# A two-layer decoder trunk on one core: who keeps the last token pairs, splits the gates and does the first u chunks of the spreading stage

## The reference

```python
q = einsum('td,dn->tn', x, wq)                      # 512 tokens, 8 heads, two halves
s1, s2 = q_half @ keys                              # 128 keys per half
v1, i1 = top_k(s1, 16); v2, i2 = top_k(s2, 16)
top_s, pos = top_k(v1[..., :, None] + v2[..., None, :], 16)
eidx = i1 * 128 + i2 at pos                         # 8 heads x 16 experts per token, of 16384
gate = softmax(top_s)
hidden = gelu(einsum('td,thkd->thk', x, u_tab[eidx]))
y = einsum('thk,thkd->td', gate * hidden, v_tab[eidx])
```

## Time and profile before

| | |
|---|---|
| time, median of 3 | 3749.36 us |
| the profiled execution, its own time | 3750.3 us |
| its span, first to last instruction | 3748.6 us |
| mean granted TensorE clock | 0.995 |
| spreading, layer 1 | about 940 to 1117 us of the span |
| spreading, layer 2 | about 2804 to 2981 us |

### The profile page before, as it was taken

How to read it: one execution, slowest core, us unless ns; L and a number is a source line. 1 busy time by engine, 2 the same in 40 slices (tenths; PEclk the granted TensorE clock), 3 DMA queues, 4 the chain that set the end, 5 groups by cost and what they waited for, 6 DMA issues and landing times. The chain is left out here.

```text
span 3748.6 us, 53748 instructions
## 1 busy us (share of the span) xinstructions
PE 3673.4 (98%) x20234; PEld 3258.1 (87%) x20234; DVE 2775.9 (74%) x4663; ACT 1488.8 (40%) x2178; POOL 1017.2 (27%) x654
## 2 busy tenths in 40 slices
PE   9999999999999999999999999999999999999999
PEld 7878888999899999888888787889999989998887
DVE  5256635499988888898862665355999798888997
ACT  2254522344763333333322545232447643333332
POOL 1000000265004555555100000002640055555541
PEclk9999999999999999999999999999999999999999
DMA  4312524354689999999832225233547899999996
GB/s 157 118 63 71 172 84 141 110 187 159 217 256 368 369 362 334 361 407 391 305 129 95 73 68 172 76 141 114 203 150 231 276 357 360 361 342 362 405 394 240
DMA packets 323828, 860.19 MB, mean 229 GB/s; under 512 B 21056, under 2 KB 119360, under 8 KB 298432
## 3 DMA queue, kind: packets, MB, share of 16 engines
q1 hardware_dynamic: 249920, 589.39, 44.0%
q0 software_dynamic: 73728, 268.47, 18.8%
HBM read 763.41 MB, written 94.37 MB: 229 GB/s over the span
## 5 line engine op out<-in xcount | busy, mean ns | idle before, releaser
L97 PE MATMUL bank<-xT_low,u_high 128*128 128x384 f32 (+1 forms) x2144 | 730.2, 341 | 19.4 <-DVEq L2104 9.5
L99 PE MATMUL bank<-xT_high,u_low 128*128 128x384 f32 (+1 forms) x2144 | 724.1, 338 | 0.0
L98 PE MATMUL bank<-xT_high,u_high 128*128 128x384 f32 (+1 forms) x2144 | 723.8, 338 | 0.0
L97 PE MATMUL bank<-v_low,w_high 128*128 128x512 f32 x1536 | 598.3, 389 | 0.4 <-DVE v_low L2131 0.3
L99 PE MATMUL bank<-v_high,w_low 128*128 128x512 f32 x1536 | 598.1, 389 | 0.0
L98 PE MATMUL bank<-v_high,w_high 128*128 128x512 f32 x1536 | 598.0, 389 | 0.0
L1325 POOL DMA_INDIRECT far_rows<-peer_u_rows_dram,far_index x256 | 369.8, 1444 | 690.5 <-DVE far_dots L1331 638.6
L1257 POOL TENSOR_TENSOR u_low<-merged,u_high 128x1024 fp32r<-128x1024 f32 x96 | 243.6, 2552 | 1098.5 <-ACT u_high L1252 1098.4
L1325 POOL DMA_INDIRECT far_rows<-peer_v_dram,far_index x256 | 385.2, 1505 | 338.9 <-DVE x_far L1349 290.4
L2043 ACT ACTIVATE v_high<-v_raw 128x1024 fp32r<-128x1024 f32 x256 | 257.1, 1052 | 453.0 <-PE bank L99 391.1
L97 PEld LDWEIGHTS bank<-xT_low,u_high 128*128 128x128 f32 x2144 | 404.3, 189 | 26.4 <-DVEq L2104 10.1
(11 more groups left out here) (451 smaller groups left out, 6772.3 us busy)
## 6 DMA issues: line engine op xcount, KB each, us to landing
merged<-peer_u_dram SPq DMA_DIRECT2D x128, 1024.0 KB, 8.0
v_raw<-peer_v_dram SPq DMA_DIRECT2D x128, 1024.0 KB, 9.1
gates_scratch<-stage SPq DMA_DIRECT2D x24, 2048.0 KB, 8.4
G<-gates_scratch SPq DMA_DIRECT2D x64, 768.0 KB, 8.2
hidden_scratch<-ahead_hid SPq DMA_DIRECT2D x72, 384.0 KB, 2.6
hid<-hidden_scratch SPq DMA_DIRECT2D x36, 768.0 KB, 8.4
mg_raw<-w_merge_dram SPq DMA_DIRECT2D x28, 768.0 KB, 4.2
merged<-w_in_dram SPq DMA_DIRECT2D x20, 1024.0 KB, 6.3
```

The source lines that it names most:

```text
L97: nc.tensor.matmul(out, lh, rl, start=first, stop=False)
L98: nc.tensor.matmul(out, lh, rh, start=False, stop=False)
L99: return nc.tensor.matmul(out, ll, rh, start=False, stop=last)
```

## The change

It has four parts, all at the two ends of spreading; every instruction's arithmetic stays what it was.

1. The copies of the last tile's pairs move from the end of routing into spreading, on ACT behind the high half of chunk 2 and ahead of the first one-hot rows. `pairs_kept` tells DVE (which waits for it before the `find` of step 16, the last tile's first) and GpSimd.
2. GpSimd, which had nothing in spreading, splits the gates of the first tile, makes `u_low` of chunks 2 and 3, and splits the gates of the other two tiles.
3. PE, ACT and DVE have u's chunks half a chunk to a chunk earlier: PE does all of chunk 2 and half of chunk 3 in step 0, then the second half of chunk n + 2 and the first half of chunk n + 3; nothing stands behind step 23, and step 23 itself has one half chunk. DVE's `low` of chunk n + 3 stands in step n from step 1 on (behind `weigh` in step 1, ahead of it from step 2). ACT's `high` of chunk n + 4 opens step n, that of chunk 4 closes step 0.
4. Each gelu is one step earlier, and with it the store of its hidden values; `keep_pairs` counts one signal per tile where it counted six.

The core of the diff:

```diff
+def keep_turned_pairs(nc, bank, rowT, listed, gateT, gate_part, t):
+
+    A = nc.scalar.activation
+    tokens = slice((t - 1) * P, t * P)
+    steps = slice((t - 1) * P // STEP, t * P // STEP)
+    by_step = bank[3][:].rearrange("p (v n s) -> p v n s", v=4, s=STEP)
+    gates = bank[3][:, 2 * P:3 * P]
+    A(rowT[:, steps, :], by_step[:, 0, :, ROWS_BY_ACT], ACT.Copy)
+    for v, first, last, at in ((1, 0, STEP, 0), (0, 0, ROWS_BY_ACT.start, STEP), (0, ROWS_BY_ACT.stop, STEP, STEP + ROWS_BY_ACT.start)):
+        A(listed[:, steps, at:at + last - first, :],
+          by_step[:, v, :, first:last].unsqueeze(3).to_broadcast([P, P // STEP, last - first, 2]), ACT.Copy)
+    A(gateT[:, tokens], gates, ACT.Copy)
+    return A(gate_part[:, tokens, :], gates.unsqueeze(2).to_broadcast([P, P, 2]), ACT.Copy)
+
+
 def route_stage(nc, a, layer, sb, sem, bank, qT, keys, x, u, load_next, ident, iota_row, rowT, listed, gateT, gate_part,
                 far):
...
             @block.scalar
...
-                keep_pairs(NT - 1)
...
+        ALREADY, FRONT = 2, 4
+        LAST_TILE = (NT - 2) * P
+
         def units_of(n):
 
-            return [(n + 1, slice(KT // 2, KT))] * (n > 0) + [(n + 2, slice(0, KT // 2))]
-
-        made = {c: max(c - 1, 0) for c in range(CHUNKS)}
-        high_at = {c - 3: c for c in range(2, CHUNKS + 2)}
-        low_at = {c - 2: c for c in range(2, CHUNKS + 2)}
+            if n == 0:
+                return [(2, slice(0, KT)), (3, slice(0, KT // 2))]
+            return [(n + 2, slice(KT // 2, KT))] + [(n + 3, slice(0, KT // 2))] * (n < STEPS - 1)
+
+        made = {c: max(c - 2, 0) for c in range(CHUNKS)}
...
+            @block.gpsimd
+            def _(pool):
+                G = nc.gpsimd
...
+                pool.sem_inc(ahead.u_low, 4)
+                split_gates(0, P, 0)
+                for c in range(ALREADY, FRONT):
+                    two_ahead(ahead.low, ahead.low_for_next, pool, c)
+                pool.wait_ge(pairs_kept, 1)
+                split_gates(P, TD, 3)
...
+                    if n * STEP == LAST_TILE:
+                        dve.wait_ge(pairs_kept, 1)
...
                 for n in range(STEPS):
                     find(n)
+                    if n >= 2:
+                        low(n)
+                    dve.wait_ge(gate_split, 3 if n < P // STEP else 6)
+                    dve.wait_ge(found, n + 1)
                     if n == 0:
-                        split_gates(0, P, 0)
-                        dve.wait_ge(gate_split, 3)
-                        dve.wait_ge(found, 1)
                         weigh(n, 0, STEP // 2)
                         weigh(n, STEP // 2, STEP)
...
-                multiply(CHUNKS + 1, slice(KT // 2, KT))
...
-                    if n in high_at:
-                        two_ahead(ahead.high, ahead.high_for_next, act, high_at[n])
+                    if n:
+                        two_ahead(ahead.high, ahead.high_for_next, act, n + FRONT)
...
-                        if g == 2 and n + 1 < CHUNKS:
-                            ahead.gelu(act, (n + 1) // EC, (n + 1) % EC)
-
-                act.sem_inc(kept, 4)
+                        if g == 2 and n == 0:
+                            ahead.gelu(act, 0, 1)
+                        if g == 2 and n + 2 < CHUNKS:
+                            ahead.gelu(act, (n + 2) // EC, (n + 2) % EC)
+                    if n == 0:
+                        two_ahead(ahead.high, ahead.high_for_next, act, FRONT)
+
+                act.sem_inc(ahead.h_act, 4)
                 act.sem_inc(stored[0], 16)
                 act.sem_inc(stored[1], 16)
-                act.sem_inc(ahead.h_act, 4)
+                ahead.high(act, 0, 2)
+                keep_turned_pairs(nc, bank, rowT, listed, gateT, gate_part, NT - 1).then_inc(pairs_kept, 1)
+                act.wait_ge(pairs_kept, 1)
+                act.sem_inc(kept, 4)
                 one_hot_rows(0)
-                two_ahead(ahead.high, ahead.high_for_next, act, high_at[-1])
+                ahead.high(act, 0, 3)
```

More of the change, by code:

```diff
@@ L1432, in turn @@
                     pe.wait_ge(sc_ready, scores_kept)
-                    pe.wait_ge(taken, 6 * t)
+                    pe.wait_ge(taken, t)
                     for j, src in enumerate((row, col, gate)):
@@ L1478, in keep_pairs @@
                     act.wait_ge(turned, 3 * t + 3)
[L1479 to L1490, removed]
+                    keep_turned_pairs(nc, bank, rowT, listed, gateT, gate_part, t).then_inc(taken, 1)
                 act.sem_inc(sc_ready, 4)
-                act.sem_inc(taken, 6)
+                act.sem_inc(taken, 1)
                 act.sem_inc(sc_free, 1)
@@ L1627, in spread_stage @@
         iota_made = sem("sp_iota_made")
+        pairs_kept = sem("sp_pairs_kept")
         gate_split = sem("sp_gate_split")
@@ L1663, in _ @@
                 V = nc.vector
-                pairs = [P, STEP, P // 2, 2]
                 def by_pairs(v):
                     return v.rearrange("p t (h two) -> p t h two", two=2)
-                def split_gates(first, last, done):
-                    shape = [P, last - first, 2]
-                    rest = gate_rest[:, first:last].unsqueeze(2).to_broadcast(shape)
[L1675 to L1679, removed]
-                    V.tensor_tensor(gate_low[:, first:last, :], rest, gate_mid[:, first:last, :], ALU.subtract).then_inc(gate_split, 1)
                 def find(n):
@@ L1697, in weigh, with low @@
                     ins.then_inc(cols_hot, (last - first) // (STEP // 2))
-                dve.sem_inc(ahead.u_low, 4)
+                def low(n):
+                    if n == 1:
+                        dve.wait_ge(ahead.u_low, 4 + FRONT - ALREADY)
+                    two_ahead(ahead.low, ahead.low_for_next, dve, n + 3)
                 V.tensor_copy(iota_pairs[:].rearrange("p h two -> p (h two)"), iota_row[:]).then_inc(iota_made, 1)
@@ L1703, in _ @@
                     find(n)
+                    if n >= 2:
+                        low(n)
+                    dve.wait_ge(gate_split, 3 if n < P // STEP else 6)
+                    dve.wait_ge(found, n + 1)
                     if n == 0:
-                        split_gates(0, P, 0)
-                        dve.wait_ge(gate_split, 3)
-                        dve.wait_ge(found, 1)
                         weigh(n, 0, STEP // 2)
                         weigh(n, STEP // 2, STEP)
-                    two_ahead(ahead.low, ahead.low_for_next, dve, low_at[n])
-                    if n:
-                        dve.wait_ge(gate_split, 3 if n < P // STEP else 6)
-                        dve.wait_ge(found, n + 1)
+                    else:
                         weigh(n, 0, STEP)
-                    if n == 2:
-                        split_gates(P, TD, 3)
-                for c in range(MADE_FIRST, EC):
-                    ahead.low_for_next(dve, c)
+                    if n == 1:
+                        low(n)
+                low(STEPS)
             @block.tensor
```

13 lines of the change are left out of this document (10 added, 3 removed).

## The result

| | before | changed |
|---|---|---|
| time, median (4 runs each) | 3749.58 us | 3774.09 us |
| lowest to highest | 3746.33 to 3750.51 | 3769.84 to 3777.56 |
| ratio, 95% interval | | 1.0063 (1.0050 to 1.0076) |
| the profiled execution, its span | 3750.3, 3748.6 us | 3769.84, 3768.1 us |
| mean granted TensorE clock | 0.995 | 0.992 |

A forecast was written before the change was run, and what follows sets the result against it. PE is busy 98% of the span, so only what moves PE counts. Per layer 10.3 - 0.5 - 2.2 = +7.6 us, +15.2 us in all, giving 3764.6 us; the forecast's own range 3757 to 3770, overall 3745 to 3770.

The forecast's parts named there:

- (1): Entering spreading: without the last pairs' copies on ACT, DVE's last `u_low` is the last arrival; gain 0.56 us per layer.
- (2): Front of spreading: PE's first chunk then ends at 944.6 us.
- (3): Front: gates on GpSimd are ready at 943.5 against 943.66 before; taking 1.1 us off DVE buys nothing.
- (4): Step 0: GpSimd's two `u_low` alternate with DVE's weighs; PE starts spreading at 950.8 after 6.2 us idle, before at 945.71.
- (6): Step 2: chunk 4's high half stands behind step 0's last copy on ACT, DVE waits; PE starts at 972.4, +10.3 us.
- The unknown price: Front: how turns are dealt; high end, one for one plus slow clock at step 2, +2.4 us per layer, not taken.
- (7): Step 3: the 0.5 us wait before it is covered, -0.5 us per layer; later steps go at PE's old pace.
- (8): End of spreading: the last half chunk no longer stands behind the last groups, -2.2 us per layer.
- (9): End: load's issue ends 5.5 us behind the store's start; idle grows to some 7 us, restart does not move, 0.
- A: Front: turns less even, DVE fits three weighs between two GpSimd turns; +7 us in all, 3756.4 us; chance 0.12.
- B: Front: DVE's bf16 instructions do not contend with GpSimd; -0.9 us per layer, 3747.5 us; chance 0.13.
- C: End: SP issues the load in 0.43 us behind the store, no slow clock; -6.9 us per layer, 3750.8 us; chance 0.08.

The follow-up runs named there:

- e1: Changed kernel with GpSimd's part undone: DVE splits the gates and makes both `u_low` of chunks 2 and 3; 3763.38 us.
- e7: Changed kernel with GpSimd making only the two `u_low` and DVE splitting the gates; 3768.8 us, run once.
- e10: Changed kernel with gelus and their stores one step later and chunk 4's high half made early, in step 0; 3755.13 us.
- e2: Changed kernel with SP's last load of u put ahead of the last store of `stage`; 3772.48 us.
- e8: Changed kernel with gates and `u_low` on DVE, gelus later, chunk 4's high half early, last load before last store, experts' two gelus moved up; 3749.97 us.
- e9: Changed kernel with the last load ahead of the last store and the experts stage's two gelus of group 1 moved up; 3775.07 us.
- e11: e8 with another deal of DVE's dot products in the experts stage, four fewer in the first two groups; 3734.91 us.
- e3: Changed kernel with every gelu of spreading, and the stores of hidden values, one step later, where they were before; 3763.32 us.
- e12: Kernel before the change with e11's deal of the dot products alone; 3747.63 us.

## Why the prediction was wrong, point by point

The sign and most of the mechanisms held, the size did not: a term was left out, and one was put at zero. Times here are from the end of the transposes, layer 1.

- (1) Entering: 0.56 us, measured 2.00 less 1.45 = 0.55. Right.
- (2), (3) Gates on GpSimd buy nothing: forecast ready at 943.5 - 938.7 = 4.8, DVE's first weigh begins at 4.5. Right, and turn for turn as said.
- (4) The two `u_low` in turns with the weighs: step 0 forecast at 12.1, measured 11.3, after 5.48 us idle where 6.2 were forecast. Right; e1 and e7 show the cause. The Trainium skill's rule that the two exclude each other for the whole instruction (SBUF — State Buffer, Who interferes with whom) holds for these bfloat16 instructions as well: 2.85 us for a 0.69 us instruction.
- (6) Chunk 4's high half as a new chain: step 2 forecast at 33.7, measured 32.8, with a wait of 2.80 us for a forecast of 3.1. Right, and shown by e10. DVE waits 5.05 us for it.
- The unknown price: I took no slow clock behind the wait before step 2, because one of 2.77 us had cost nothing before. It came, in both layers (granted clock 0.70 in 970 to 975): half of the 2.9 us that PE ran in it, 1.5 us per layer. This was the high end, taken for zero.
- (7) "From there on a step is PE's and goes at its old pace." **This is the step that failed.** I had listed that each gelu comes a step earlier, and costed it at nothing without asking what a gelu waits for. It waits for the store of the values that it overwrites, and that store sits on SP behind the store of `stage` and a load, now held 4.9 us. Price: 3.50 us idle and 1.7 us of slow clock in layer 1, 2.41 us in layer 2.
- (8) The half chunk, -2.2 us: inside the sum below, not shown by itself.
- (9) The end: idle near 7 us and a load of 4.9 us, measured 6.91 and 4.92. Right. The reading given with it, that the queue takes the load once the store's packets have drained, does not hold: in the kernel before, the last store's 4096 packets run from 1.2 to 7.4 us behind its start, and the load's issue ends at 5.5, with over a quarter of them to come. What ends it there is open.

The sum for layer 1: 7.6 forecast, less 0.9 for step 2, plus 1.5, 3.5 and 1.7 is 13.4; the last store is 13.4 us later. For layer 2, where step 2 starts at 32.2: 7.6 - 1.5 + 1.5 + 2.4 = 10.0; measured 10.1. That is 23.5 us at the two last stores, in profiled executions that differ by 19.5 us. Layer 1 enters spreading 1.4 us earlier in the changed one, and gives back 2.7 us between its last store and the last transposes of layer 2, 1.2 of them by PE's 200th matmul, since 2.9 us of slow clock fall behind its restart in place of 5.4. The other 5 us, between the profiled execution and the median of the changed kernel, no profile shows.

Of the rivals, A fails (turns are one for one) and B fails (the bfloat16 instructions do contend). C's mechanism was tried in e2: the idle fell to 2.2 us as C says once the load is not held, but C's gain of 6.9 us per layer did not come. C took the slow clock for gone, and it came behind 2.20 us of idle too. And C took a shorter idle for time saved. With the load first, the store lands later: SP's next load, which waits for the stores, is issued 8.4 us behind the last store before and 10.2 us behind it in e8 (1124.12 and 1123.48). ACT then waits 1.3 to 6.4 us for v in e2, e8, e9 and e11 where in the others it does not wait, and DVE's queue stands behind that. This chain I had not read. Had the load been quick in the changed kernel, the forecast for C would have been wrong.

What stays open: why the changed kernel's runs lie 7.7 us apart, and what part of the 27 to 29 us between the last store and the first dot product could be cut. Loading v before the store lands was not tried.

## What to carry to other kernels

Before an instruction is moved up a queue, list everything it waits for, also what was always long done, such as a store that frees its buffer: a step earlier it may be the last to arrive. An idle stretch ahead of a stage is worth its length only if nothing else sets that stage's pace; here, once PE restarted early, the work of DVE hung on the landing of the last store, and repairs worth 6 us per layer showed only when DVE was relieved too. And work given to GpSimd beside a busy DVE cost DVE about the length of GpSimd's instruction: two subtractions of 1.2 us on DVE became two holds of 2.2 us on instructions that PE was waiting for.

## What the runs showed of the hardware that was not expected

- A GpSimd CAST with one input, of 256 elements, is held by DVE's `find` as well: 2.07 us at 938.91, against 0.95 us for one of 512 elements at 948.02.
- Whether the granted clock falls to its half around step 2 does not follow from PE's idle time there. In the changed kernel it fell in both layers (2.80 and 2.77 us), again in e1 and e3; in the kernel before it stayed at 1.00 behind 2.77 us in both. e12 has both in one execution, behind 2.80 us each, step 2 of layer 2 and of layer 1:

```profile
2816.00:2821.00 5.00, 3.86 (x31) 3.89 (x32) 5.00 (x4) 1.82 (x6) 0.00 (x0) 0.66 0.36 149
954.00:959.00 5.00, 4.67 (x43) 4.71 (x44) 5.00 (x5) 3.00 (x7) 0.00 (x0) 1.00 0.20 84
```

  It stayed full behind 2.80 us in e9 (1.00 in 969 to 974, layer 1) and fell behind 2.20 us in e2. An idle time of that length is no safe side, and one idle that cost nothing does not price the next.
- From the last store of `stage` to DVE's first dot product it is 26.9 to 29.0 us in all 13 profiles and both layers, while PE's restart moves from 1.5 to 6.5 us behind that store. Two chains of nearly one length make it: where the load of u stands behind the store, DVE follows PE's restart and v has landed in time; where the load stands first, ACT and DVE wait for v.
